# A two-layer hybrid decoder step on one Trainium2 core: layers unrolled, ring-freeing matmuls dropped, norm squares added on VectorE, FFN norm factor applied after the matmuls

## The reference

```python
x = x + 0.5 * ((silu(h @ wg) * (h @ wu)) @ wd)          # FFN 1, h = rmsnorm(x, ffn1_norm)
h = rmsnorm(x, mix_norm); z = h @ w_in                  # mixer: dilated attention, short conv, sparse attention
x = x + (sum_i sigmoid(h @ w_gate)_i * (branch_i @ w_branch_i)) @ w_out
x = x + 0.5 * ((silu(h @ wg) * (h @ wu)) @ wd)          # FFN 2, h = rmsnorm(x, ffn2_norm)

def rmsnorm(x, g):
    y = x * rsqrt(mean(x * x, axis=-1) + 1e-6)
    return y * g
```

## Time and profile before

| what | value |
|---|---|
| device time, median of 3 runs | 2790.09 us (2778.65 to 2804.6) |
| span of the profiled execution | 2770.2 us |
| median less that span | 19.9 us |
| PE busy | 2569.1 us (93%), 10662 matmuls |
| DVE / ACT / POOL busy | 974.1 / 529.2 / 282.6 us |
| mean granted TensorE clock | 0.940 of full speed |
| moved by DMA | 382.32 MB, mean 138 GB/s |

### The profile page before, as it was taken

One profiled execution on the slowest core, in us unless ns is written; L12 is line 12 of the kernel. 1 busy time (PEld: TensorE's weight loads), 2 busy tenths in 40 slices (PEclk: granted clock), 3 DMA queues, 4 the chain that ended last, 5 costly groups with the idle time before them and its releaser, 6 DMA issues.

```text
span 2770.2 us, 33525 instructions
## 1 busy us (share of the span) xinstructions
PE 2569.1 (93%) x10662; PEld 1682.6 (61%) x10662; DVE 974.1 (35%) x1706; ACT 529.2 (19%) x1030; POOL 282.6 (10%) x532
## 2 busy tenths in 40 slices
PE   7998899998889899999989998999988898999998
PEld 4665467654446566666656664776544565566666
DVE  1001355755556441200010014766455654411000
ACT  2100221133321231111011003211323113311100
POOL 3430000000011120000342000000000202100000
PEclk9999999999999788999999998999899997789999
DMA  5474237363535341233435621573555343323332
GB/s 162 148 235 139 96 131 270 109 244 126 170 114 158 92 122 46 97 117 116 138 117 199 215 81 66 202 277 109 169 170 168 128 131 92 90 79 104 115 113 65
DMA packets 317953, 382.32 MB, mean 138 GB/s; under 512 B 23902, under 2 KB 300967, under 8 KB 316139
## 3 DMA queue, kind: packets, MB, share of 16 engines
q1 hardware_dynamic: 292290, 257.40, 29.9%
q0 software_dynamic: 19712, 118.79, 12.1%
q10 hardware_dynamic: 5800, 4.30, 0.5%
HBM read 374.80 MB, written 92.91 MB: 169 GB/s over the span
## 4 chain that ended last, share of the span: by engine, by line
PE 86%; DVE 5%; DMA 3%; issue 3%; ACT 3%; SPq 0%; DVEq 0%; ACTq 0%
PE ps L617 46%; PE ps L673 11%; PE ps L901 4%; PE ps L905 4%; PE ps L864 3%; PE ps L873 3%; PE ps L838 2%; PE ps L841 2%; PE ps L891 1%; PE ps L782 1%; PE ps L716 1%; DMA ring<-in_ffn_wd 1%; PE ps L726 1%; PE ps L813 1%; ACT pT L1015 1%
## 5 line engine op out<-in xcount | busy, mean ns | idle before, releaser
L617 PE MATMUL ps<-h,ring 128*128 128x320 f32 x3200 | 896.1, 438 | 21.3 <-DVE h L1291 17.8
L617 PEld LDWEIGHTS ps<-h,ring 128*128 128x128 f32 x3200 | 604.4, 191 | 265.2 <-DVE h L1291 11.4
L617 PE MATMUL ps<-area,ring 128*128 128x320 f32 x1280 | 356.1, 436 | 12.6 <-DMA ring<-in_ffn_wd 4.9
L673 PE MATMUL ps<-ring,h 128*128 128x256 f32 (+3 forms) x1440 | 323.0, 384 | 10.6 <-DVE h L1291 7.8
L617 PEld LDWEIGHTS ps<-area,ring 128*128 128x128 f32 x1280 | 244.0, 191 | 114.5 <-issue 10.3
L673 PEld LDWEIGHTS ps<-ring,h 128*128 128x128 f32 (+1 forms) x1440 | 244.6, 178 | 79.6 <-issue 22.2
L1299 DVE TENSOR_TENSOR area<-silu,ps 128x320 f32 x64 | 31.2, 488 | 539.3 <-ACT silu L1040 539.3
L356 POOL DMA_DIRECT2D area<-in_cache_c_idx x256 | 137.6, 538 | 496.0 <-issue 480.7
L373 POOL DMA_DIRECT2D area<-in_cache_c_kv x176 | 97.9, 556 | 743.7 <-issue 743.7
L1015 ACT ACTIVATE kT<-ps 128x512 f32<-128x512 f32 (+3 forms) x248 | 126.0, 544 | 197.9 <-PE ps L841 117.6
L1306 DVE SCALAR_TENSOR_TENSOR x<-ps,x 128x320 f32<-128x320 f32 x48 | 23.6, 492 | 364.4 <-PE ps L617 364.4
(11 more groups left out here) (185 smaller groups left out, 2129.3 us busy)
## 6 DMA issues: line engine op xcount, KB each, us to landing
out_s_a_kv<-in_cache_a_kv POOLq DMA_DIRECT2D x64, 1020.0 KB, 8.2
ring<-in_w_in SPq DMA_DIRECT2D x80, 512.0 KB, 4.7
ring<-in_ffn_wg SPq DMA_DIRECT2D x64, 512.0 KB, 4.4
ring<-in_ffn_wu SPq DMA_DIRECT2D x64, 512.0 KB, 4.5
ring<-in_ffn_wd SPq DMA_DIRECT2D x64, 512.0 KB, 5.2
area<-in_cache_a_kv SPq DMA_DIRECT2D x32, 1024.0 KB, 6.5
ring<-in_w_gate SPq DMA_DIRECT2D x48, 512.0 KB, 4.6
area<-in_cache_c_kv POOLq DMA_DIRECT2D x176, 128.0 KB, 2.8
```

Source lines behind the costliest of these rows:

```text
L617: last = mm(bank(b, T), w[:, j, c0:c0 + P], rhs[:, j, :], start=(j == 0), stop=(j == k - 1))
L673: last = mm(dst, h3[:, k, t0:t0 + rows], w[:, k, :], start=(k == 0), stop=(k == KD - 1))
```

## The change

- The layer loop and the loops inside it are written out on all engines; semaphore targets are constants.
- `used` and `unit_used` go. A load now waits for the semaphore that the unit's last real matmul counts up anyway (`last_use`): `gu_ready` for gate and up units (it counts once per half, so both units of a pair are freed at the end of the pair), `down_ready`, `z_proj`, `b_ready` or `m_ready` for the others.
- ACT still squares each chunk, but DVE adds squares 0 to 6 up (`add_square`, six additions per norm), and PE does two multiplications per norm instead of eight, both after the projection (`mean_square`).
- For the two FFNs h is x * gain without the row factor (`gained`), written chunk by chunk as x becomes ready. DVE multiplies each gate block and each up block by rs as it leaves PSUM, ACT takes the silu of the scaled gate in SBUF, and DVE multiplies the two. The mixer's norm stays as it was.
- The rows of the next layer's gains are loaded, turned and copied during FFN 2 of the layer before; in SP's queue they stand after a wait for the last x chunk of w_out and ahead of FFN 2's weights. In layer 0 PE turns the rows before it turns x. The 12 loads of head gains have a semaphore of their own and stand behind the weights of FFN 1.
- The first cache copies are paced by `gu_ready` (from 8, then 4 per batch) instead of `unit_used` (from 10, then 6 per batch).

```diff
+        def last_use(q):
+            for f, q0 in ((0, FFN1), (1, FFN2)):
+                if q0 <= q < q0 + 16:
+                    return gu_ready, f * KF + 2 * ((q - q0) // 2) + 2
+                if q0 + 16 <= q < q0 + 24:
+                    return down_ready, 2 * f * KD + q - q0 - 15
...
-                    sp.wait_ge(unit_used.sem, unit_used.at(l, q - SLOTS + 1) + 8 * i)
-                    alone(sp)
+                    before = before_in_slot(q)
+                    if l or before >= 0:
+                        done, n = last_use(before % LAYER)
+                        sp.wait_ge(done.sem, done.at(l if before >= 0 else l - 1, n))
...
+                if l + 1 < DEPTH:
+                    sp.wait_ge(x_ready.sem, x_ready.at(l, 2 * KD))
+                    load_rows(l + 1)
                 load_ffn(FFN2, a["ffn2_wg"], a["ffn2_wu"], a["ffn2_wd"])
...
-                moves(0, 2, unit_used, 10, 6, 4)
+                moves(0, 2, gu_ready, 8, 4, 4)
...
-            def mean_square(l, n, k):
-                pe.wait_ge(sq_ready.sem, sq_ready.at(l, (n - 1) * KD + k + 1))
-                ins = mm(bank(6, T), ones[:, :], squares[k], start=(k == 0), stop=(k == KD - 1))
-                if k == KD - 1:
-                    ins.then_inc(ms_ready.sem, 1)
+            def mean_square(l, n):
+                pe.wait_ge(sq_summed.sem, sq_summed.at(l, n))
+                mm(bank(6, T), ones[:, :], squares[KD - 2], start=True, stop=False)
+                pe.wait_ge(sq_ready.sem, sq_ready.at(l, n * KD))
+                mm(bank(6, T), ones[:, :], squares[KD - 1], start=False, stop=True).then_inc(ms_ready.sem, 1)
...
-                def used(q):
-                    n = 1
-                    while q + n in PADS:
-                        n += 1
-                    mm(ps[0:32, 4095:4096], cbf("ident")[:, 0:32], cbf("ident")[:, 0:1], start=True, stop=True
-                       ).then_inc(unit_used.sem, n)
...
-                            fn(silu[:, e * T:(e + 1) * T], bank(2 * e, T), ACT.Silu).then_inc(silu_ready.sem, 1)
+                            act.wait_ge(gate_scaled.sem, gate_scaled.at(l, f * KF + e + 1 + 2 * i))
+                            fn(silu[:, e * T:(e + 1) * T], silu[:, e * T:(e + 1) * T], ACT.Silu).then_inc(silu_ready.sem, 1)
...
+            def gained(k, n):
+                ts(h3[:, k, :], x3[:, k, :], vec[:, n * KD + k:n * KD + k + 1], None, ALU.mult).then_inc(h_ready.sem, 1)
+            def add_square(l, n, k):
+                dve.wait_ge(sq_ready.sem, sq_ready.at(l, (n - 1) * KD + k + 1))
+                ins = tt(squares[k], squares[k - 1], squares[k], ALU.add)
+                if k == KD - 2:
+                    ins.then_inc(sq_summed.sem, 1)
+                else:
+                    step(ins)
...
-                            dve.wait_ge(silu_ready.sem, silu_ready.at(l, f * KF + e + 1) + 2 * i)
-                            tt(hid[:, bass.ds((2 * i + e) * T, T)], silu[:, e * T:(e + 1) * T], bank(2 * e + 1, T), ALU.mult
-                               ).then_inc(hid_ready.sem, 1)
+                            dve.wait_ge(gu_ready.sem, gu_ready.at(l, n))
+                            tt(silu[:, e * T:(e + 1) * T], bank(2 * e, T), rs[:, :], ALU.mult).then_inc(gate_scaled.sem, 1)
+                            tt(dst, bank(2 * e + 1, T), rs[:, :], ALU.mult).then_inc(up_scaled.sem, 1)
+                            dve.wait_ge(up_scaled.sem, up_scaled.at(l, n))
+                            dve.wait_ge(silu_ready.sem, silu_ready.at(l, n))
+                            tt(dst, silu[:, e * T:(e + 1) * T], dst, ALU.mult).then_inc(hid_ready.sem, 1)
...
                         stt(x3[:, c, :], bank(4 + c % 2, T), scale, x3[:, c, :], ALU.mult, ALU.add).then_inc(x_ready.sem, 1)
+                        if n == 1 or (n == 2 and l + 1 < DEPTH):
+                            dve.wait_ge(x_ready.sem, x_ready.at(l, n * KD + c + 1))
+                            gained(c, 2 if n == 1 else 0)
+                        if c >= 2:
+                            add_square(l, n + 1, c - 1)
```

More of the change, by code:

```diff
@@ L114, in __call__, with before_in_slot @@
         ins.then_inc(self.count.sem, 1)
[L115 to L124, removed]
+        self.eng.wait_ge(self.count.sem, self.n)
+def before_in_slot(q):
+    p = q - SLOTS
+    while p % LAYER in PADS:
+        p -= SLOTS
+    return p
 def unit_order(q):
@@ L413, in load_ffn @@
                 def load_ffn(q0, wg, wu, wd):
[L414 to L417, removed]
+                    for v in range(8):
+                        load(q0 + 2 * v, w_k8(wg, v * 256))
+                        load(q0 + 2 * v + 1, w_k8(wu, v * 256))
                     for c in range(KD):
@@ L498, in _ @@
                 load_a(0, 0, kbuf3, ak_in)
-                with sp.Fori(0, NB - 1) as b:
+                for b in range(0, NB - 1):
                     sp.wait_ge(sj_kturned.sem, sj_kturned.at(l, 4) + b * 4)
@@ L524, in _ @@
             pool.wait_ge(consts_in.sem, 48)
-            with pool.Fori(0, DEPTH) as l:
+            for l in range(0, DEPTH):
                 pool.wait_ge(x_ready.sem, x_ready.at(l, 1 - KD))
@@ L540, in moves @@
                 def moves(b0, n, pace, first, each, gap):
-                    with pool.Fori(0, n) as b:
+                    for b in range(0, n):
                         for part in range(MOVES):
@@ L590, in _, with arrived @@
                 last.then_inc(turned_in.sem, 1)
[L591 to L604 removed]
+            mean_square(0, 0)
+            for l in range(0, DEPTH):
+                def arrived(q):
                     s = slot_in[q % SLOTS]
[L606 removed]
+                    pe.wait_ge(s.sem, s.at(l, 32 * unit_order(q)))
                 def tiles(q, k, n):
@@ L921, in sample_jobs @@
                     if kind == "a":
-                        with pe.Fori(0, NB // 2 - 1) as i:
+                        for i in range(0, NB // 2 - 1):
                             two(i)
@@ L943, in merge @@
                                 at += 1
-                            used(q)
                             q += 1
-                pe.wait_ge(rows_in.sem, rows_in.at(l, rows_in.per_layer))
-                alone(pe)
-                tr(bank(7, 36), vrows[0:36, :], ident[0:36, 0:36])
-                for c in range(4):
-                    last = tr(bank(7, 16, at=64 + 16 * c), srows[0:16, c * P:(c + 1) * P], ident[0:16, 0:16])
-                last.then_inc(vec_turned.sem, 1)
                 ffn(0, FFN1)
@@ L1026, in _ @@
             squares_of_x(0, 0)
-            with act.Fori(0, DEPTH) as l:
+            for l in range(0, DEPTH):
                 def norm(n):
@@ L1152, in _ @@
                 turn(IDX_UNITS - 1)
-                with act.Fori(0, 2) as i:
+                for i in range(0, 2):
                     for e in range(2):
@@ L1224, in sample_jobs @@
                     keys(0)
-                    with act.Fori(0, NB // 2 - 1) as i:
+                    for i in range(0, NB // 2 - 1):
                         one(2 * i, 0)
@@ L1280, in _, with root, norm @@
             dve.wait_ge(consts_in.sem, 48)
-            with dve.Fori(0, DEPTH) as l:
-                step = Steps(dve, steps, l)
-                def norm(n):
-                    if n == 0:
-                        dve.wait_ge(vec_ready.sem, vec_ready.at(l, 1))
+            step = Steps(dve, steps)
+            def gained(k, n):
[7 more added lines that the diff above has]
+                    step(ins)
+            dve.wait_ge(vec_ready.sem, vec_ready.at(0, 1))
+            for k in range(KD):
+                dve.wait_ge(x_ready.sem, k + 1 + x_ready.prime - KD)
+                gained(k, 0)
+            for k in range(1, KD - 1):
+                add_square(0, 0, k)
+            for l in range(0, DEPTH):
+                def root(n):
                     dve.wait_ge(rms_ready.sem, rms_ready.at(l, n + 1))
                     step(nc.vector.reciprocal(rs[:, :], rs[:, :]))
+                def norm(n):
+                    root(n)
                     for k in range(KD):
@@ L1557, in sample_jobs @@
                     scores(0, 0)
-                    with dve.Fori(0, NB // 2 - 1) as i:
-                        step.loop(i, 4 + 4 * rounds_each)
+                    for i in range(0, NB // 2 - 1):
                         one(2 * i, 0)
                         one(2 * i + 1, 1)
-                    step.end(NB // 2 - 1)
                     one(NB - 2, 0, True, False)
@@ L1585, in _ @@
                 index_setup()
-                with dve.Fori(0, 2) as i:
+                for i in range(0, 2):
                     for e in range(2):
@@ L1621, in _ @@
                 ffn(1)
-                assert step.n == steps.per_layer, ("DVE steps in a layer", step.n)
 OUTPUTS = (("y_prompt", (1, 256, 1024)), ("y_sample", (8, 8, 1024)),
```

109 lines of the change are left out of this document (63 added, 46 removed).

## The result

The changed kernel takes 2693.76 us (median of 4 runs, 2688.5 to 2708.51) beside 2784.37 us for the kernel before (4 runs, 2774.46 to 2804.6): ratio 0.967, with a 95% interval of 0.9624 to 0.9716. The forecast was 2702 us. The profiled execution of the changed kernel took 2688.5 us with a span of 2686.8, so no more than 1.7 us lies around a span. The stretch from the mixer's first conv block to the first block of its branches, which holds the prompt jobs, took 607 to 630 us for both layers of one and the same code from profile to profile, the longest where the granted clock was lowest. So experiments are compared by the stages outside it, and their totals by the medians and ratios. One execution of the experiments (2782.95 us, with the tiny matmuls put back) was in a slower state of the chip; its ratio leaves it out, its median does not.

What follows compares the result with a forecast made beforehand. PE, busy 93% of the span and carrying 86% of the last-ending chain, was taken as the bound. Terms summed to -88 us, span 2770.2 to 2682, plus 19.9 making 2702 us; range 2660 to 2745.

Steps and rivals of the forecast that it cites:

- Slot-freeing matmuls, -50: Dropping 180 tiny PE matmuls, 166 of them counted at 0.30 us each, saves 50 us; bounds 16 to 54.
- The rival by which the gaps stay: Block boundaries cost the same with or without the slot-freeing matmul: 16 us saved instead of 50, time 2736; chance 0.13.
- Mean squares, -20: Between down blocks in six projections, six mean squares each leave PE's path at 0.55 us: 20 us saved.
- FFN 1 of layer 1, -12: At its start, 10.5 us saved because h needs no root and weights are there, plus 1.5 of the slow first run.
- FFN 2, +1: Start after w_out stays bound by its weights' load: half a microsecond gained in layer 1, 1.4 lost in layer 0.
- Mixer's norm, +1: The norm before the mixer keeps its whole chain and gets a longer multiplication: 0.5 us more each, 1 in all.
- the ends of gate and up, +2: One scaling by rs (0.49 us) joins the silu and product chain PE waits for: 2 us more for four ends.
- Start, -4.4: At the kernel's start rows are turned before x, so FFN 1 starts near 31: 4.4 us saved, between 2 and 7.
- Copies, -3: Weight loads beside cache copies: layer 0's burst stall changes by -3 us, between -8 and +8; layer 1 0, at worst +8.
- joints give less: Layer 0's burst starves two more units (+16 us) and layer 1 gets a stall (+8): time 2726; chance 0.15.
- Registers and branches, -3: Constant semaphore targets take some of the chain's 78 us of "issue": 3 us saved, between 0 and 35.
- The time around the span, 19.9: The median time was taken to lie 19.9 us above the profiled span, turning span 2682 into 2702 us.

Runs made afterwards that it cites:

- the fastest run: Changed kernel with each layer's first two cache-copy batches moved to FFN 2, and FFN 2's first weights reusing slots freed by w_out's first units: 2658.79 us, ratio 0.9535.

## Why the prediction was right, point by point

The time was right to 8 us, and the direction and most of the reasons held. That the sum fits so well is in part luck: the terms were not all right, and misses of opposite sign cancel.

- **Slot-freeing matmuls, -50.** Right in size: 0.30 us each, and 50 to 57 us by the two runs that put them back. Wrong in the step that explained it ("the gap on either side, when PE leaves float32 and comes back"): in float32 they cost 0.35. The rival by which the gaps stay is out. (The lower bound of 16 is half of all 180; half of the 29 in its own working is 15.)
- **Mean squares, -20.** Measured some 17: 0.50 us instead of 0.55 for each, less at joints.
- **FFN 1 of layer 1, -12.** FFN 2's down part to this start fell by 87.77 - 71.83 = 15.9 us; less seven tiny matmuls between blocks (2.1; with them put back this stretch takes 73.96) and the mean squares (2.3 here) 11.5 are left. The start came 1.18 us after the mean square. The run with unrolling alone shares it out: 5.55 for the loop's turn, and by subtraction the rest for h without a root.
- **FFN 2, +1.** Less its mean squares (the experiment that puts them back), w_out to FFN 2 stands at 45.47 and 43.01 beside 44.65, of which some 0.9 are three slot-freeing matmuls that only the kernel before has: +1.7 and -0.7, where +1.4 and -0.5 were worked out. What was said to be late next, the weights' load behind w_out's slots, is what the fastest run took away.
- **Mixer's norm, +1, and the ends of gate and up, +2.** Last down block to mixer 5.85 us (261.20 to 267.06), and 5.79 before (264.02 to 269.81), so nothing for the norm; the wait at the end of FFN 1's gate and up went from 1.15 to 1.68, 0.5 as worked out.
- **Start, -4.4.** FFN 1 starts at 30.44 and not 35.41: -5.0.
- **Copies, -3, "between -8 and +8" and 0 in layer 1, "at worst +8": the step that failed.** Measured +12.1 in layer 0 (20.3 against 8.2) and +6.3 in layer 1, the second inside its bound and the first outside. The step took POOL to reach the copies "no earlier than now" and PE to be "some 12 us further, with two down units loaded before the burst". The two units were loaded, but POOL's pages, unrolled, go out faster, and the first copy left at 168.02 instead of 176.46; the down projection began at 171.70 instead of 181.31, so against the burst PE had gained 1.2 us and not 12. Two blocks are 17.5 us of work, and the third unit's load, which had left 0.7 us ahead of the first copy, left 2 us behind it and took 36.87 us. Two parts of the change that let this happen had been named (slots freed in pairs, a pace that lets two batches go at once) and each was costed alone, at nothing; the third, POOL's faster pages, was not foreseen. The price to take stood in the profile, landings of up to 33.3 us: from an issue near 170 the unit lands near 203, 14 us after it is needed. The rival "joints give less" had the mechanism, and its +16 and +8 are near what was measured.
- **Why a copy ahead costs so much.** In the burst the two queues moved packet for packet, 279 each in 26 us of the changed kernel and 224 each from 184 to 204 us of the kernel before. The Trainium skill ("DMA: Bandwidth & Descriptors", section on queues, rings and completion order) has each DMA engine take turns between queues packet by packet. The trace agrees. The prediction's estimate of 25 us for a unit of 1 MB took packets of 0.88 and 6.0 KB, the means over the whole kernel; in the burst they are 0.50 and 29.6 KB, so a unit hardly moves until the copies are through, and that 25 was near the 26.9 and 33.3 us of the earlier trace rows is chance. What sets the landing is the burst's own length: 10.7 MB at the 324 GB/s of this stretch are 33 us, from 168 to 201. The 36.87 and 38.2 us in the burst fit that, against a median of 5.3 us for a down load over the whole kernel.
- **Registers and branches, -3.** Too small. Unrolling alone takes 5.9 and 3.9 us out of the token units (in that stretch of layer 0, 290 to 420 us, the pieces of the chain put down to "issue" go from 6.6 to 3.3 us), beyond the loop's turn that was counted elsewhere. Some -10 is shown; in the prompt jobs nothing can be told, as their clock varies from profile to profile.
- **The time around the span, 19.9.** A wrong step that cost little: it is 1.7 us. The median of the kernel before lay 19.9 above the profiled span because that execution (2771.9 with the same 1.7) was shorter than the four timed ones.

So copies came out some 21 us worse (+18.4 against -3), registers and branches about 7 us better outside the prompt jobs, and the rest lies in sizes of a few microseconds and in the mixers. With these sizes the terms add up to about -72; of the 12 us that are missing to -83.4, 7 lie in the two mixers (39.6 less 22.8 for tiny matmuls and 9.8 for the token units). What gave them was not found.

## What to carry to other kernels

A matmul that only signals costs more than its busy time: price it from start to start with and without it, and let the last useful matmul carry the semaphore. Before dropping it, look at what its earlier signal set off, since a slot that comes free 4 us later can put a weight load behind a burst of copies, where it takes seven times as long. Where a large background transfer shares the DMA engines with a short ring, put it where the ring has slack and pace it; costing the ring's loads by their median there is the mistake; the price is the time that the burst ahead takes to get through, its bytes over the rate that the queues move.

## What was not expected of the hardware

- A tiny float32 matmul of two MATMULs between float32 blocks costs 0.35 us, one in bfloat16 0.30: the gap does not come from changing precision. What it does come from stays open.
- Beside the burst the copies' and the weights' queue got the same number of packets through, 279 and 279, so bytes went by packet size, 8.26 against 0.14 MB.
- A DMA issue can itself hold the issuing queue: 29.22 us here while the loads ahead of it were starved, with everything behind it on SP waiting too.
- POOL's DMA issues, 0.54 us each, stand 1.14 us apart unrolled and 1.23 us in a loop; 0.09 us in each of some 130 issues moved the burst by 12 us, and a wait of 4.9 us was gone with it in the kernel before; a slot freed 4 us later goes with a wait of 18.2 us instead of 10.9 in the changed one.
